# Moving four modulation groups from layer 0's queries to VectorE in a four-layer diffusion backbone step

## The reference

```
shift, scale, gate = split(silu(cond) @ ada_w[l] + ada_b[l], 3)   # cond: c_ctx for context, c for latents
h = rms_norm(x, norm_pre[l]) * (1 + scale) + shift
o = mixer(h)            # projections from 2048, mixing, a SiLU gate path, output projection to 2048
x = x + gate * rms_norm(o, norm_post[l])
```

## Time and profile before

| | us |
|---|---|
| median of three runs | 3120.0 (3116.55 to 3123.25) |
| the profiled execution | 3118.98 |
| its span | 3117.2 |
| PE busy | 2915.5 (94%) |
| DVE busy | 1961.5 (63%) |
| ACT busy | 1043.0 (33%) |
| POOL busy | 513.3 (16%) |

### The profile page before, as it was taken

One profiled execution on the slowest core, in us unless ns is written; L12 is line 12 of the kernel. 1 busy time (PEld: TensorE's weight loads), 2 busy tenths in 40 slices (PEclk: granted clock), 3 DMA queues, 4 the chain that ended last, 5 costly groups with the idle time before them and its releaser, 6 DMA issues.

```text
span 3117.2 us, 46268 instructions
## 1 busy us (share of the span) xinstructions
PE 2915.5 (94%) x18667; PEld 2556.9 (82%) x18667; DVE 1961.5 (63%) x4112; ACT 1043.0 (33%) x1399; POOL 513.3 (16%) x421
## 2 busy tenths in 40 slices
PE   5799999999899999889998999999988999999998
PEld 2588889978678999879877877987777999987777
DVE  4499987745576666748685673764387774235443
ACT  1433333233324222232324334223324223323332
POOL 2034443100152110005352000000153000000000
PEclk7899999999999999999999999999999999999999
DMA  9899996621385897777685342553385665331142
GB/s 375 327 315 355 355 347 220 236 81 41 126 300 206 231 255 274 274 284 272 237 316 176 127 157 95 216 190 108 103 318 209 212 221 172 125 95 55 55 162 95
DMA packets 243429, 648.12 MB, mean 208 GB/s; under 512 B 22592, under 2 KB 56096, under 8 KB 217616
## 3 DMA queue, kind: packets, MB, share of 16 engines
q1 hardware_dynamic: 215232, 524.58, 48.3%
q0 software_dynamic: 27984, 120.59, 10.9%
HBM read 573.07 MB, written 71.97 MB: 207 GB/s over the span
## 4 chain that ended last, share of the span: by engine, by line
PE 71%; DVE 11%; DMA 6%; ACT 4%; issue 2%; DVEq 2%; POOL 1%; ACTq 1%; SPq 0%; POOLq 0%
PE bank L363 35%; PE bank L367 18%; DMA raw<-in_ada_w 3%; PE bank L956 3%; PE bank L950 3%; DVE w_lo L562 2%; DVE arena L2240 2%; PE bank L971 2%; PE bank L997 1%; ACT hT_hi L631 1%; PE bank L975 1%; DMA raw<-in_mla_w_in 1%; ACT w_hi L546 1%; PE bank L1549 1%; PE bank L2578 1%
## 5 line engine op out<-in xcount | busy, mean ns | idle before, releaser
L546 ACT ACTIVATE w_hi<-raw 128x2048 fp32r<-128x2048 f32 (+2 forms) x352 | 520.2, 1496 | 1168.8 <-PE bank L363 616.5
L363 PE MATMUL bank<-hT_hi,w_hi 128*128 128x384 f32 (+1 forms) x2608 | 885.7, 340 | 24.1 <-DVEq L563 9.6
L363 PE MATMUL bank<-hT_hi,w_lo 128*128 128x384 f32 (+1 forms) x2608 | 875.7, 336 | 0.0
L363 PE MATMUL bank<-hT_lo,w_hi 128*128 128x384 f32 (+1 forms) x2608 | 875.6, 336 | 0.0
L562 DVE TENSOR_TENSOR w_lo<-raw,w_hi 128x2048 fp32r<-128x2048 f32 (+3 forms) x289 | 473.2, 1656 | 462.6 <-ACTq L547 455.4
L363 PEld LDWEIGHTS bank<-hT_hi,w_hi 128*128 128x128 f32 (+1 forms) x2608 | 491.5, 188 | 41.4 <-issue 23.3
L363 PEld LDWEIGHTS bank<-hT_lo,w_hi 128*128 128x128 f32 (+1 forms) x2608 | 491.8, 189 | 1.2
L363 PEld LDWEIGHTS bank<-hT_hi,w_lo 128*128 128x128 f32 (+1 forms) x2608 | 491.2, 188 | 1.0
L367 PE MATMUL bank<-w_hi,hT_hi 128*128 128x512 f32 x1056 | 419.6, 397 | 35.1 <-POOL w_lo L554 24.1
L367 PE MATMUL bank<-w_lo,hT_hi 128*128 128x512 f32 x1056 | 416.3, 394 | 0.0
L367 PE MATMUL bank<-w_hi,hT_lo 128*128 128x512 f32 x1056 | 416.1, 394 | 0.0
(11 more groups left out here) (345 smaller groups left out, 2859.7 us busy)
## 6 DMA issues: line engine op xcount, KB each, us to landing
raw<-in_ada_rows SPq DMA_DIRECT2D x128, 1024.0 KB, 6.2
raw<-in_ada_w SPq DMA_DIRECT2D x64, 1024.0 KB, 8.9
raw<-in_mla_w_in SPq DMA_DIRECT2D x64, 768.0 KB, 7.6
raw<-in_gla_w_in SPq DMA_DIRECT2D x48, 1024.0 KB, 5.1
raw<-in_mla_w_in SPq DMA_DIRECT2D x40, 1024.0 KB, 5.2
raw<-in_mla_w_out SPq DMA_DIRECT2D x32, 1024.0 KB, 5.2
raw<-in_s_w_in SPq DMA_DIRECT2D x32, 1024.0 KB, 8.2
s_out_dram<-arena POOLq DMA_DIRECT2D x32, 512.0 KB, 5.9
```

Source lines behind the costliest of these rows:

```text
L363: mm = nc.tensor.matmul(banks[m][0:width, 0:TOK], wp[:, k, at:at + width], hp[:, kt, :], start=(first and n == 0), stop=(last and n == 2))
L546: nc.scalar.activation(dst, src_, ACT.Copy)
```

## The change

- `ADA_TENSOR` is 12: groups 8 to 11 stay on PE, hosted by query groups 0, 2, 4 and 6; groups 12 to 15 become DVE's set 0, and the later sets move on by one stage. GLA's set has eight groups (32 to 39): 128 steps where there were 64. r0 and r2 host 16 each, where they hosted none; vb 20 where it hosted 8.
- For the sets of out0, out1, out2 and GLA the SiLU is spread by PE straight into banks 4 and 5 (`pe_silu`, 32 products with the identity, 128 columns by 32 wide), after the first chunk; POOL's fetch and DVE's copies go for those.
- In out0 to out2 DVE splits chunk 1, POOL moves the gates ahead of the load of x, and nothing of the SiLU is fetched there.
- S5 preparation: the first columns (L2258, L2279) and the copy of bank 2 (L1292) go from DVE to ACT in layer 0.
- krope and glr use bank 3. The second chunk of u1 and q3 is split within the normalisation, after the second quarter of h. Sets 3 and 5 are taken earlier.

```diff
-ADA_TENSOR = 16
-ADA_READ = (7, 11, 15)
+ADA_TENSOR = 12
+ADA_READ = (7, 11)
...
-    return {("q0", g): ADA_START + g for g in range(ADA_TENSOR - ADA_START)}
+    return {("q0", 2 * g): ADA_START + g for g in range(ADA_TENSOR - ADA_START)}
...
-    gla = {("qa2", 0): (2, 2, 2, 2), ("ka2", 0): (2, 2, 2, 2), ("va2", 0): (2, 2, 0, 0), ("r1_2", 0): (3, 3, 3, 3),
-           ("qb2", 0): (3, 3, 3, 3), ("kb2", 0): (3, 3, 3, 3), ("vb2", 0): (3, 3, 2, 0)}
+    gla = {("qa2", 0): (3, 3, 3, 3), ("ka2", 0): (2, 2, 2, 2), ("va2", 0): (1, 1, 1, 1), ("va2", 1): (1, 1, 1, 1),
+           ("r0_2", 0): (4, 4, 4, 4), ("r1_2", 0): (4, 4, 4, 4), ("qb2", 0): (3, 3, 3, 3), ("kb2", 0): (3, 3, 3, 3),
+           ("vb2", 0): (3, 3, 3, 3), ("vb2", 1): (2, 2, 2, 2), ("r2_2", 0): (4, 4, 4, 4), ("r3_2", 0): (4, 4, 0, 0)}
...
+        def pe_silu(pe, f, conditions=(0, 1)):
+
+            pe.wait_ge(ada_turned, set_taken(f) - 1)
+            for c in conditions:
+                for j in range(4):
+                    for q in range(4):
+                        mm = nc.tensor.matmul(banks[4 + c][32 * q:32 * q + 32, j * P:(j + 1) * P],
+                                              silu_c[:, 4 * q + j, c:c + 1].broadcast_to([P, 32]), ident[:, :],
+                                              start=True, stop=True, skip_group_check=True)
+            mm.then_inc(pe_spread, 1)
...
-            first, end = {"gate0": (3, 10), "out0": (1, 16), "glu1": (2, 16), "out1": (1, 16), "out2": (1, 16)}.get(name, (99, 99))
-            return first <= 4 * g + s < end and (name[:3], 4 * g + s) != ("out", 2)
+            first, end = {"gate0": (3, 10), "out0": (3, 16), "glu1": (2, 16), "out1": (3, 16), "out2": (3, 16)}.get(name, (99, 99))
+            return first <= 4 * g + s < end
...
                 split_h("act", [q])
                 if q == 0 and l % 3 == 2:
                     split_chunk("act", f"glr{l}", 0, 1)
+                if q == 1 and l % 3 != 2 and l != layers[0]:
+                    split_chunk("act", f"{'qu'[l % 3]}{l}", 0, 1)
...
         def fetch_x(pool, l):
 
             pool.wait_ge(h_lo_ready, h_quarter(f"mix{l}", 3))
-            if l != layers[-1]:
-                pool_silu(pool, (1, 4, 5)[l])
-            if l == 1:
-                pool.wait_ge(ada_turned, set_taken(3))
+            pool_gates(pool, l)
...
-                v.tensor_copy(wb_[d][:, :, 7 - 7 * d, :], bc[hb % 2][:, 128 * d:128 * d + 128].rearrange("p (a q) -> p a q", q=SC))
...
+        def act_s5_in_firsts(act, hb):
+
+            if hb == 0:
+                x_free(act, 0)
+            else:
+                act.wait_ge(s5_turned, 4 * hb)
+            act.wait_ge(bc_in[hb % 2], 16 * (hb // 2 + 1))
+            for d in range(2):
+                cp = act_copy(wb[:, d, :, :, 112 - 112 * d:128 - 112 * d].rearrange("p r g q -> p (r g) q"),
+                              bc[hb % 2][:, 128 * d:128 * d + 128].rearrange("p (a q) -> p a q", q=SC))
+            cp.then_inc(s5_w_ready, 1)
...
-                if l != layers[-1]:
-                    pool_splits(f"out{l}", 1, 2)
                 fetch_x(pool, l)
-                pool_gates(pool, l)
```

More of the change, by code:

```diff
@@ L93, in banks_used, with banks_of @@
     return 4
+def banks_of(name):
+    return range(3, 4) if banks_used(name) == 1 else range(banks_used(name))
 def chunks_of(name):
@@ L117, in summed_sets @@
     out_place = (12928, 13632, 13448, 14144)
[L118 to L123, removed]
+    return [evenly(range(12, 16), chunks("gate0", 0, 15)) + ((13824, 14336, 22144, 13824),),
+            evenly(range(16, 20), chunks("out0", 1, 14)) + (out_place,),
+            evenly(range(20, 24), chunks("u1", 1, 16) + chunks("gate1", 0, 11)) + ((4608, 5120, 5632, 4608),),
+            evenly(range(24, 28), chunks("glu1", 1, 15)) + ((19200, 19712, 20224, 19200),),
+            evenly(range(28, 32), chunks("out1", 1, 14)) + (out_place,),
+            (range(32, 40), [key + (s,) for key, counts in gla.items() for s in range(4) for _ in range(counts[s])],
              (12928, 13632, 13448, 12928)),
@@ L350, in group_sums @@
                 hi, lo = (w[:, slot, :, :] if tiles_in == 4 else all_tiles(w[:, slot, :, :], P) for w in (w_hi, w_lo))
-                for m in range(banks_used(name)):
+                for n_tile, m in enumerate(banks_of(name)):
                     if s == 0 and taken_before(name, g, m):
@@ L422, in pe_ada_take, with sums_of @@
             pe.wait_ge(ada_turned, set_taken(f) - 1)
[L423 to L426, removed]
+            for first in range(0, len(groups), 4):
+                for k in range(4):
+                    mm = nc.tensor.matmul(banks[5][32 * k:32 * k + 32, 8 * first:8 * first + 32], spread[:, :],
+                                          sums_of(f, first)[:, k, :], start=True, stop=True, skip_group_check=True)
             mm.then_inc(ada_turned, 1)
-        def sums_of(f):
-            return view(SETS[f][2][2], 4, 32)
+        def pe_silu(pe, f, conditions=(0, 1)):
[7 more added lines that the diff above has]
+            mm.then_inc(pe_spread, 1)
+        def sums_of(f, n):
+            return view(SETS[f][2][2], 4, 32) if n < 4 else a8_words[:, 384:512].rearrange("p (k n) -> p k n", k=4)
         def silu_placed(f, c):
@@ L579, in split_next @@
                 split_chunk(eng, *dense[n])
+        SPLIT_IN_NORM = [f"{('q', 'u', 'glr')[l % 3]}{l}" for l in layers if l != layers[0]]
         def stream(eng, name, write=None, between=None, ahead=None):
@@ L592, in stream @@
                         dve_ada_step(a, k)
-                    if s == 1 and name[:3] == "glr":
+                    if (g, s) == (0, 1) and name in SPLIT_IN_NORM:
                         pass
@@ L796, in between @@
                     if (g, s) == (0, 0):
+                        if l != layers[-1]:
+                            pe_silu(pe, (1, 4, 6)[l])
                         pe_turn_gates(pe, l)
@@ L1468, in turning @@
                 return between
-            group_sums(pe, f"glr{l}", 0, [2 * GRANK], bank_wait=first_banks(l), inputs=f"norm{l}")
+            group_sums(pe, f"glr{l}", 0, [2 * GRANK], bank_wait=first_banks(l), inputs=f"norm{l}",
+                       between=lambda s: pe_silu(pe, 5) if s == 0 else None)
             group_sums(pe, f"qa{l}", 0, [P] * 4, between=qa_between)
@@ L1835, in dve_gla @@
             dve_unit(dve, 3)
-            stream("dve", f"r3_{l}", None, lambda g, s: gate(2, s - 1) if s < 3 else None)
+            stream("dve", f"r3_{l}", None, lambda g, s: gate(2, s - 1) if s < 3 else dve_ada_take(5) if s == 4 else None)
             split_h("dve", [0], g_res)
@@ L2326, in act_s5_turned, with act_s5_out_firsts @@
                          banks[6 + g % 2][:, :].rearrange("p (c h n) -> p c h n", c=4, h=2)).then_inc(s5_turned_copied, 1)
+        def act_s5_in_firsts(act, hb):
+            if hb == 0:
+                x_free(act, 0)
+            else:
+                act.wait_ge(s5_turned, 4 * hb)
[4 more added lines that the diff above has]
+            cp.then_inc(s5_w_ready, 1)
+        def act_s5_out_firsts(act, hb):
+            if hb >= 2:
+                act.wait_ge(s5_ca_stored[hb % 2], 16 * 2 * (hb // 2))
+            for d in range(2):
+                for r in range(2):
+                    at = 256 + 128 * d + 64 * r
+                    cp = nc.scalar.activation(ca[hb % 2][:, d, r, :, 128 * d:128 * d + SC],
+                                              bc[hb % 2][:, at:at + 64].rearrange("p (g q) -> p g q", g=4), ACT.Copy,
+                                              scale=-1.0 if r else 1.0)
+            cp.then_inc(s5_c_ready, 1)
         def act_s5_blocks(act, hb):
             act.wait_ge(bc_in[hb % 2], 16 * (hb // 2 + 1))
[L2330 removed]
+            act.wait_ge(s5_w_ready, 2 * (hb + 1))
             for g2 in range(2):
```

89 lines of the change are left out of this document (45 added, 44 removed).

## The result

The changed kernel takes 3132.4 us (median; 3123.5 to 3137.7), the kernel before 3119.6 (3115.7 to 3126.0) beside it: a ratio of 1.0035, 95% interval 1.0025 to 1.0046. That is 13 us slower, where 3113 was forecast: the prediction was wrong, on the other side of "no change", and the time lies just outside its range, which reached to 3132.

What follows compares the result with a forecast made beforehand. DVE paces layer 0's queries, PE and a DVE-ACT exchange bound GLA, POOL's late split causes the out-stage gaps. Queries -15, GLA +29.4, vb +4.5, out stages -23, small -3 make -7: 3120 to 3113, range 3096 to 3132.

Steps and rivals of the forecast that it cites:

- Out0 to out2: Output stages: gates ahead of x remove PE's gaps at chunk 3; gains 10, 6 and 7 us, together -23.
- the small ones: Minor changes in q3, u1, qa and elsewhere: together with va -3 us, bounds -5 and +2.
- out stages move their gap to chunk 4: Rival, out0 to out2: chunk 4's load lands late beside POOL's 5 MB; 5 us more per stage, 3128 in all; chance 0.12.
- Queries: Layer 0's queries: work taken from DVE cuts a block from 18.48 to 17.8 us; with fewer groups, -15 us.
- four turns of 0.9: Layer 0's queries: one item in PE's sum for a block with hosted groups, 17.5 to 18.4 us.
- GLA: r0 and r2: 16 hosted steps each, ahead of work the unit waits for, add 14.7 us each, +29.4.
- the steps followed through r0: r0: first delay hidden, then splits 4.5 (4.6 with the wait) and 9.7 us later, unit's second half 14.7 later.
- vb: GLA, second group of vb: two hosted steps per chunk delay the unit by 4.5 us, bounds 0 and 7.
- The gate store: Out0 to out2: issued ahead of x, POOL's small store lands in 2 to 4 us, freeing POOL before chunk 3.
- `pe_silu`: Out0 to out2: PE's 64 instructions spreading the SiLU cost 1.8 us per stage, bounds 0 and 4.
- Second chunk of q3: q3: its 3.04 us wait is relieved by an earlier split, but the first chunk is delayed 1.75; net -1.2 us.
- The first rival: r0, r2 and vb: hosted steps fit into DVE's idle time and cost nothing, 3079, or 3096 if half; chance 0.16.

Runs made afterwards that it cites:

- x_late: Kernel after, but POOL issues the load of x in out0 to out2 only behind its splits of chunks 3 to 7, gates still first; 3110.1 us, ratio 0.9966.
- x_first_c1: Kernel after, but in out0 to out2 POOL splits chunk 1, then issues the load of x, then the gates; 3128.3 us, ratio 1.0026.
- x_first: Kernel after, but POOL issues the load of x ahead of the gates in out0 to out2, as before; 3109.7 us, ratio 0.9963.

## Why the prediction was wrong

**The step that failed** is the one in "Out0 to out2" that reads "What is late next is the load of chunk 4, beside the broadcast and the load of x: about 1 us". It was the load, as said, but the price was 20 us over three stages (the sum for out2 even leaves the 1 us out). Forecast were 10, 6 and 7 us of gain; measured were 4.9, -1.8 and -0.5. By the sum, -15 + 29.4 + 4.5 - 2.6 with nothing for the small ones is +16, and the span shows +15.8.

Why 1 us was wrong: I priced the load alone. Three things came with its lateness. SP's loads take 13.2 us in the median, the weights and the rows alike; DVE stands idle 8.2 us before rows that take 13.11 to land, with the bank copy L1296 queued behind its steps; and PE, which needs that bank, stands 5.9 to 6.4 us and comes out of it at a lower granted clock. The rows for it were at hand: the load of x takes 16.7 us when it runs beside the refills, so its 3 MB and the broadcast's 2 take the engines for longer than the one chunk that the ring was ahead.

**The rival "out stages move their gap to chunk 4"** described this, with its point of decision (a landing of over 10 us; 13.1 was measured) and 5 us per stage, and had 0.12. Its price was too low by 2 per stage, which also left its total at 3128. In the crowded 20.3 us the rows of the queues show 544 packets of POOL and 750 of SP. POOL's packets are 9.6 KB on average and SP's 3.7, so POOL has 66% of the bytes. It leaned on a rule of the Trainium skill, "DMA: Bandwidth & Descriptors", "Queues, rings and completion order": the DMA engines take turns between queue rows packet by packet. The trace agrees roughly: the packets stand 0.7 to 1, the bytes 1.9 to 1. I had read the rule as "evenly", and that was too kind to SP.

**What held.**
- Queries: -12.9 for -15, by the mechanism named. In the sum for PE's block, "four turns of 0.9" is a slip: it would give 19.1 to 19.9, more than the block lasts. The trace has two such turns (L2303, x8 each), which give 17.3 to 18.1, so the conclusion stands. The block is 17.8 us as forecast, without hosted groups, and 18.0 with one.
- GLA: r0 +15.8 and r2 +14.5 (72.0 for 57.5) for 14.7 each, r1 to r2 with vb +3.4 for 4.5. Each of the steps followed through r0 came out within 0.4 us. What r0 has over 14.7 stands behind that point and is PE's clock in the unit, 22.35 us for 21.22 (below). In the vb stretch the unit starts 5.0 later, and 1.6 come back by a better clock in it.
- The gate store: "2 to 4 us" was right (2.7), and so was the gap at chunk 3 going.
- `pe_silu`: 1.88 us for 1.8.
- Second chunk of q3: its wait of 3.04 is gone, the first chunk's is 3.16 for 1.42.

**The first rival** ("the steps fit into DVE's idle time") was rightly held against the order in the code, but it held the larger lesson: one edit away lay 36 us.

The rest of the account is noise or open. Layer 1 is 3.6 us longer (571.8 for 568.2, from the end of out0's run to the first product of out1), but in the eight variants in which nothing there differs from the kernel after it takes 567.2 to 577.4. What of the 3.6 belongs to the change wasn't separated, nor was the -3.5 behind out2.

## What to carry to other kernels

Work that is hosted in an engine's idle time costs nothing only where it stands behind everything that the bound engine waits for: count the idle time, then read the order in which the instructions stand. When a wait is taken out of a queue, look at what is released with it: here the freed wait sent 5 MB into the microseconds in which the ring was refilled, and a big load belongs either into a stretch in which the DMA engines stand idle (0.21 busy here, 10 us earlier) or where the consumer is several chunks ahead. A loss found this way can be worth more than the change: here the two orders gave 61 us, and the change as made cost 13.

## What the runs showed of the hardware

- Beside POOL's 5 MB, SP's 1 MB loads landed in 13.2 us (median, up to 15.6); in the like stretch of x_late, beside the 2 MB of the gates but without the 3 MB, in 5.9. The engines moved 395 GB/s meanwhile. Of POOL's and SP's packets 42% were POOL's, of their bytes 66%.
- A 16 KB store behind a 3 MB load in POOL's queue landed in 13.8 us (median, x_first_c1), with nothing ahead of it in 2.7, and issued 4 to 7 us after the load in 6.6 (x_first).
- The 32 products with the identity of `pe_silu`, 64 instructions of 128 columns by 32 wide in float32, took 1.88 us on PE in out0 and out1 and 1.89 in out2, 29 ns each.
- PE's granted clock behind a gap of the out stages. The windows of 8 us behind out2's last gap, 6.19 us long in the kernel after and 1.01 in x_first:
```profile
2301.04:2309.04 8.00, 8.00 (x24) 6.37 (x25) 7.93 (x25) 0.00 (x1) 4.59 (x1) 0.67 0.92 345
```
```profile
2282.46:2290.46 8.00, 8.00 (x35) 6.62 (x36) 7.93 (x25) 1.78 (x1) 4.64 (x1) 1.00 0.76 272
```
24 matmuls begin at a clock of 0.67 and 35 at 1.00: 11 matmuls of 0.23 us are 2.5 us per gap, beside the gap; 0.82 and 29 were read before. Behind the gaps of out0 and out1 in the kernel after, the same windows show 0.76 with 27 and 0.62 with 23.

In GLA the clock behind a wait is not one price. The same piece of r0, from the first product of the unit's second half to the first product of r1, in the kernel before (a wait of 1.89 ahead of it), in the kernel after (14.58) and in x_late (14.57, with the same GLA):
```profile
1925.19:1946.41 21.22, 21.10 (x82) 11.54 (x83) 3.85 (x9) 6.09 (x15) 1.44 (x2) 0.84 0.12 50
```
```profile
1925.08:1947.43 22.35, 22.23 (x82) 12.21 (x83) 3.86 (x9) 6.09 (x15) 1.46 (x2) 0.79 0.12 48
```
```profile
1907.52:1926.74 19.22, 19.11 (x82) 10.26 (x83) 3.86 (x9) 6.09 (x15) 1.46 (x2) 0.93 0.14 58
```
1.00 is the 2.4 GHz level throughout; a value between is a mixture of it with 1.2 GHz. In the five traces with the GLA of after this piece takes 19.2 to 22.4 us in r0, behind practically the same wait, and in r2 19.3 to 19.4. So up to 3 us of such a stage are chance of the single trace. In vb the piece is 21.3 at 0.84 in both traces with the GLA of before, 19.6 to 19.8 with that of after, and 18.0 at 1.00 in all four with DVE's own work first; why it is steady there was not followed up.
